# Selection stage of a two-layer encoder kernel: up products over both halves of h at once, in four PSUM banks

## What is computed

```
q  = h @ w_query                                # 8 heads x 128
s1, s2 = q halves times sub_keys                # 128 scores each, per token and head
t1, i1 = top_k(s1, 16);  t2, i2 = top_k(s2, 16)
top_s, top_c = top_k(t1[:, None] + t2[None, :], 16)       # 16 of 256 candidates
experts = i1[top_c // 16] * 128 + i2[top_c % 16];  gates = softmax(top_s)
act = gelu(h . expert_u[experts]);   out = sum(gates * act * expert_v[experts])
```

## Time and profile before

| | us |
|---|---|
| Median of 3 runs (lowest, highest) | 2142.79 (2142.04, 2148.08) |
| The profiled execution | 2141.82 |
| Its span, first to last instruction | 2140.0 |

### The profile page before, as it was taken

The page is one execution under the profiler, slowest core; times in us unless marked ns, Lnnn a source line. Parts: engine busy times, 40 slices in busy tenths (PEclk is TensorE's granted clock), DMA queues, the critical chain, the costliest instruction groups (busy, mean ns, idle before and its releaser), DMA issues.

```text
span 2140.0 us, 38983 instructions
## 1 busy us (share of the span) xinstructions
PE 2045.1 (96%) x12710; PEld 1750.0 (82%) x12710; DVE 1494.8 (70%) x2924; ACT 991.5 (46%) x1651; POOL 665.2 (31%) x548
## 2 busy tenths in 40 slices
PE   7999999988999999999999999998899999999997
PEld 5764899877888999999867549998778899999996
DVE  7882777787778666666678737778877776666665
ACT  4542454575346444444344435446643554444443
POOL 3993466763000000000059916667610000000000
PEclk9999999999999999999999999999999999999998
DMA  5212554203558555555423145542045665555553
GB/s 184 99 70 118 183 173 165 99 21 100 194 190 297 187 186 186 186 187 186 137 95 109 50 160 177 174 159 80 11 152 192 221 196 187 188 186 188 188 186 109
DMA packets 90542, 329.41 MB, mean 154 GB/s; under 512 B 10531, under 2 KB 14755, under 8 KB 88140
## 3 DMA queue, kind: packets, MB, share of 16 engines
q1 hardware_dynamic: 90428, 328.18, 45.2%
q10 hardware_dynamic: 16, 0.02, 0.0%
HBM read 324.99 MB, written 3.16 MB: 153 GB/s over the span
## 4 chain that ended last, share of the span: by engine, by line
PE 73%; POOL 12%; issue 8%; DVE 2%; DMA 2%; ACT 1%; POOLq 1%; DVEq 0%; ACTq 0%; SPq 0%
PE ps L782 33%; PE ps L803 32%; POOL arena L1721 7%; POOL v_raw L1721 3%; PE ps L813 3%; PE ps L746 3%; POOL u_raw L1721 2%; PE ps L698 1%; DVE arena L1259 1%; DMA v_raw<-in_expert_v 1%; PE ps L868 1%; DMA arena<-in_keys 1%; DVE v_hl L1259 1%; PE ps L824 0%; ACT v_hl L1104 0%
## 5 line engine op out<-in xcount | busy, mean ns | idle before, releaser
L803 PE MATMUL ps<-v_hl,w_hl 128*128 128x512 f32 x3072 | 731.0, 393 | 7.5 <-DVE v_hl L1259 7.3
L803 PEld LDWEIGHTS ps<-v_hl,w_hl 128*128 128x128 f32 x3072 | 567.0, 189 | 126.8 <-DVE v_hl L1259 11.2
L782 PEld LDWEIGHTS ps<-h_hl,u_hl 128*128 128x128 f32 x4800 | 598.3, 192 | 12.7
L782 PE MATMUL ps<-h_hl,u_hl 128*128 128x256 f32 x4800 | 608.0, 284 | 0.0
L1721 POOL TENSOR_TENSOR arena<-arena 128x256 f32<-128x256 f32 (+1 forms) x240 | 197.9, 863 | 615.8 <-DVE arena L1259 614.6
L1104 ACT ACTIVATE v_hl<-v_raw 128x1024 fp32r<-128x1024 f32 x208 | 220.8, 1062 | 319.1 <-PE ps L803 292.9
L1259 DVE TENSOR_TENSOR u_hl<-u_raw,u_hl 128x1024 fp32r<-128x1024 f32 x148 | 182.7, 1234 | 188.4 <-ACT u_hl L1066 185.9
L1066 ACT ACTIVATE u_hl<-u_raw 128x1024 fp32r<-128x1024 f32 x144 | 152.9, 1062 | 239.9 <-PE ps L782 239.0
L1259 DVE TENSOR_TENSOR v_hl<-v_raw,v_hl 128x1024 fp32r<-128x1024 f32 x208 | 253.8, 1220 | 12.4 <-ACT v_hl L1104 12.4
L782 PE MATMUL ps<-h_hl,v_hl 128*128 128x256 f32 x1344 | 171.6, 285 | 0.1
L782 PEld LDWEIGHTS ps<-h_hl,v_hl 128*128 128x128 f32 x1344 | 164.8, 192 | 1.7 <-issue 0.5
(11 more groups left out here) (173 smaller groups left out, 2344.7 us busy)
## 6 DMA issues: line engine op xcount, KB each, us to landing
u_raw<-in_expert_u SPq DMA_DIRECT2D x208, 512.0 KB, 3.3
v_raw<-in_expert_v SPq DMA_DIRECT2D x208, 512.0 KB, 3.3
v_raw<-in_expert_u SPq DMA_DIRECT2D x48, 512.0 KB, 4.1
u_raw<-in_expert_v SPq DMA_DIRECT2D x48, 512.0 KB, 3.3
arena<-in_w_in SPq DMA_DIRECT2D x16, 512.0 KB, 3.6
arena<-in_w_in SPq DMA_DIRECT2D x8, 1024.0 KB, 5.1
arena<-in_ssm_b SPq DMA_DIRECT2D x16, 512.0 KB, 4.3
arena<-in_w_out SPq DMA_DIRECT2D x4, 2048.0 KB, 9.6
```

Source lines behind the costliest of these rows:

```text
L782: m = pe.matmul(ps[:, bank, o:o + S], hl[:, wp, k, :], h_hl[:, hp_, k, :], start=(k == 0 and j == 0), stop=(k == DC - 1 and j == 2))
L803: m = pe.matmul(ps[:, 2 * a + half, :], w_hl[s][:, wp, a * P:(a + 1) * P], v_hl[s][:, vp, half * 512:(half + 1) * 512], start=(first and j ...
```

## The change

- **PE** (`up_wide`). The high part of a u slice is multiplied with both halves of `h` by one matmul of 512 columns, into a whole bank: columns 0 to 255 collect high by high, columns 256 to 511 high by low. The low part of the slice adds its 256-column product to columns 0 to 255. An early up product is then 8 matmuls of 512 and 8 of 256 columns, in place of 24 of 256. Each writes one of four banks, and waits for the sum of product `c - 4`. The ahead products stay as they were.
- **ACT** (`half_early`). It copies columns 256 to 511 into row `c` of `gates`. GELU runs three tiles later, in place on that row. The last three GELUs follow behind the last head.
- **DVE** (`pre_early`). It adds columns 0 to 255 to the row. The 48 additions stand between the steps of the selection, six to a head, two tiles behind; the last two stand ahead of the memset that raises `s_topd`.
- The loops on DVE and ACT are turned and unrolled to fit; DVE's loop body now holds two heads.

```diff
 MAG_BANK = 3
+EARLY_BANK = (4, 5, 2, 3)
 TURN_BANK = 0
...
+        def up_wide(c, hl, bank):
+            pe.wait_ge(s_u_lo, l * PK + c + 1)
+            both = ps[:, bank, :].rearrange("p (r t) -> p r t", r=2)
+            def high(k):
+                return pe.matmul(both, hl[:, 0, k, :], h_hl[:, :, k, :], start=(k == 0), stop=(k == DC - 1))
+            high(0)
+            for k in range(DC - 1):
+                pe.matmul(ps[:, bank, 0:S], hl[:, 1, k, :], h_hl[:, 0, k, :], start=False, stop=False)
+                if k < DC - 2:
+                    high(k + 1)
+            pe.matmul(ps[:, bank, 0:S], hl[:, 1, DC - 1, :], h_hl[:, 0, DC - 1, :], start=False, stop=False)
+            high(DC - 1).then_inc(s_u_mm, 1)
         def up_early(c, k):
-            pe.wait_ge(s_gelu, 2 + l * PK + c - 1)
-            up(c, early_hl[k], 4 + k % 2, 0)
+            pe.wait_ge(s_pre_early, l * EARLY + c + 1)
+            up_wide(c, early_hl[k], EARLY_BANK[k])
...
         up_ahead(EARLY + 1, 1, early_hl[1])
+        pe.wait_ge(s_pre_early, 4 + (l + 1) * EARLY)
         pe.wait_ge(s_sel, l + 1)
...
-        def gelu_early(c, s):
+        def half_early(c, k):
+            act.wait_ge(s_u_mm, 2 + l * PK + c + 1)
+            act.activation(gates[:, bass.ds(c, 1), :].rearrange("p o t -> p (o t)"),
+                           ps[:, EARLY_BANK[k], S:2 * S], ACT.Copy).then_inc(s_half, 1)
+        def gelu_early(c):
             act.drain()
-            act.wait_ge(s_u_mm, 2 + l * PK + c + 1)
+            act.wait_ge(s_pre_early, 4 + l * EARLY + c + 1)
             fenced(ACT.Gelu)
-            act.activation(gates[:, bass.ds(c, 1), :].rearrange("p o t -> p (o t)"), ps[:, 4 + s, 0:S],
-                           ACT.Gelu).then_inc(s_gelu, 1)
+            row = gates[:, bass.ds(c, 1), :].rearrange("p o t -> p (o t)")
+            act.activation(row, row, ACT.Gelu).then_inc(s_gelu, 1)
...
                     high_ahead(j - HEAD_UPS + 3)
-                gelu_early(c, j % 2)
+                half_early(c, k % 4)
+                if not first or j >= 3:
+                    gelu_early(c - 3)
                 if following and j == 2:
...
         high_early(2, 2, 0, False)
+        head(0, 0, True, 0, first=True)
         with act.Fori(0, PH // 2 - 1) as hp:
-            head(hp * 2, 0, True, hp * 3)
             head(hp * 2 + 1, 1, True, hp * 3)
-        head(PH - 2, 0, True, 3 * PH // 2 - 3)
+            head(hp * 2 + 2, 0, True, hp * 3 + 3)
         head(PH - 1, 1, False, 3 * PH // 2 - 3, last=True)
+        for c in range(EARLY - 3, EARLY):
+            gelu_early(c)
...
-        with dve.Fori(0, PH) as h:
+        def pre_early(c, k):
+            dve.wait_ge(s_half, l * EARLY + c + 1)
+            row = gates[:, bass.ds(c, 1), :].rearrange("p o t -> p (o t)")
+            tt(row, row, ps[:, EARLY_BANK[k], 0:S], ALU.add).then_inc(s_pre_early, 1)
+        def head(h, s, first):
+            def pre(j):
+                if not first or j >= 2:
+                    pre_early(h * HEAD_UPS + j - 2, (s * HEAD_UPS + j + 2) % 4)
             ih = l * PH + h
...
                 .then_inc(s_sc_used, 1)
+            pre(0)
             dve.drain()
             dve.tensor_copy(i16, i16u)
             tt(cand, t16[:, 0, :, :].unsqueeze(3).broadcast_to([P, TT, 16, 16]),
                t16[:, 1, :, :].unsqueeze(2).broadcast_to([P, TT, 16, 16]), ALU.add)
+            pre(1)
             dve.drain()
             cf = [cand[:, a, :, :].rearrange("p i j -> p (i j)") for a in range(TT)]
             top16(cf, [cand2[:, a, :] for a in range(TT)], [top[:, a, :] for a in range(TT)],
                   [cu[:, a, :] for a in range(TT)])
+            pre(2)
             dve.drain()
...
                top[:, :, 0:1].broadcast_to([P, TT, TOPK]), ALU.subtract)
+            pre(3)
             dve.drain()
             dve.tensor_copy(rank, rank_u)
             dve.drain()
             tt(pick_r, rank_f.unsqueeze(2).broadcast_to([P, 4 * TOPK, TOPK]), over(iota16, 4 * TOPK), ALU.is_equal)
+            pre(4)
             dve.drain()
...
                                   pick[:, b, :, :, :], AX.X, ALU.add)
-            dve.drain()
+            pre(5)
+            dve.drain()
+        dve.wait_ge(s_spill, 16 * (l + 1))
+        head(0, 0, True)
+        with dve.Fori(0, PH // 2 - 1) as i:
+            head(i * 2 + 1, 1, False)
+            head(i * 2 + 2, 0, False)
+        head(PH - 1, 1, False)
+        for c in (EARLY - 2, EARLY - 1):
+            pre_early(c, c % 4)
         dve.memset(fence[:, 2:3], 0.0).then_inc(s_topd, 1)
```

More of the change, by code:

```diff
@@ L317, in encoder @@
         s_gelu = sem("s_gelu")
+        s_pre_early = sem("s_pre_early")
+        s_half = sem("s_half")
         s_wt = sem("s_wt")
@@ L1133, in copy_scores, with head @@
                         .then_inc(s_sc_sb, 1)
-                def head(h, s, following, nth, last=False):
+                def head(h, s, following, nth, last=False, first=False):
                     for j in range(HEAD_UPS):
@@ L1245, in _ @@
             dve.sem_inc(s_gates, 4)
+            dve.sem_inc(s_pre_early, 4)
             for counter in (s_u_mm, s_v_mm, s_gelu, s_pp, s_drive):
```

## The result

The changed kernel takes 2147.16 us (median of 14 runs, 2145.89 to 2149.25), the kernel before 2144.06 us on the same chip (median of 14, 2138.86 to 2148.08). The ratio is 1.0016, with a 95% interval of 1.0009 to 1.0024: it is slower by 3 us. The forecast was 2139.0 us and a small gain. The range held the time, the sign was wrong. The profiled execution of the changed kernel took 2149.25 us, its span is 2147.4 us against 2140.0 before.

A forecast was written before the change was run, and what follows sets the result against it. PE was taken to bound the selection stage. 2141.82 − 9.0 (products) + 5.2 (waits at the end of two layers) = 2138.0 us profiled; with the median 0.97 us above, 2139.0 us was predicted, 8-of-10 range 2132 to 2157.

The forecast's parts named there:

- the sign: Whole kernel: a small gain forecast; chances given were faster 0.20, same 0.55, slower 0.25.
- What bounds the kernel: Selection stage: PE, busy 180.79 of 182 us, sets the pace; DVE has about 4.9 us slack a head.
- PE's part: Early up products: 2786 ns instead of 2880, 94 ns saved each, 9.0 us for 96 products.
- The first rival: Mixed stream of widths saves nothing; products stay at 2.88 us, 2146.7 us in all; chance 0.17.
- the larger saving: Rival on PE's products: fixed matmul cost half hidden, 4.5 us more saved, 2134.5 or 2132 us; chance 0.18.
- DVE's additions: Selection heads: 0.34 us an addition, six make 2.0 us a head, 18.7 us, hidden behind PE's 21.0.
- The end of the stage: Ahead of the transposes: selection ready 8.3 us after product 47, PE waits 2.6 us, 5.2 for two layers.
- The last head: DVE's last head in the selection stage: 20.85 us plus 2.04 for six additions, ending 4.1 us after product 47.
- The chain behind it: After DVE's last head: additions 0.7 us, one GELU 0.48, table load 1.28, exponentials 0.42, then DVE's three steps.
- The exposed table load: End of the selection stage: load for the exponentials, 1.28 us, formerly in DVE's shadow, now behind the last GELU.
- The sum for the profiled execution: Whole kernel: 2141.82 − 9.0 + 5.2 = 2138.0 us.
- The second rival: Selection stage: DVE becomes the bound through losing to POOL; 2167 us, or 2149 if milder; chance 0.25 for both.

The follow-up runs named there:

- x2: Changed kernel with each early up product's eight wide matmuls first, then its eight narrow ones: 2150.61 us, ratio 1.0038 to the kernel before.
- x9: Changed kernel with two small operands of DVE's selection (ranks, first indices) cast into PSUM bank 7: 2131.53 us, ratio 0.9941 to the kernel before.
- x1: Changed kernel with early up products again in 24 matmuls of 256 columns, ACT's copies and DVE's additions kept: 2151.7 us, ratio 1.0032 to the kernel before.
- x5: Changed kernel with s_topd raised before additions 45 to 47, and exponentials before the last three GELUs: 2144.7 us, ratio 1.0007 to the kernel before.
- x4: Changed kernel with eleven idle matmuls of 256 columns ahead of PE's wait for the selection: 2147.91 us, ratio 1.0022 to the kernel before.
- x7: Changed kernel with the last six products of a layer done as before, the other 42 wide: 2134.62 us, ratio 0.9964 to the kernel before.
- x10: Kernel before, with the same two operands in PSUM as x9: 2142.84 us, ratio 0.9992 to the kernel before.
- x12: x9 and x5 together, on the changed kernel: 2134.16 us, ratio 0.9948 to the kernel before.
- x13: x12 with the eight wide matmuls of a product first, as in x2: 2136.86 us, ratio 0.9955 to the kernel before.
- x15: x9 and x7 together, on the changed kernel: 2136.0 us, ratio 0.9951 to the kernel before.

## Why the prediction was wrong, step by step

**What bounds the kernel** held: PE sets the pace, and DVE has little slack left (its heads take 19.6 to 20.6 us in the middle of the stage, up to the end of the reductions, inside the 18.7 to 21.0 us given).

**PE's part** held in kind. The saving is 75 ns a product by the heads (60 by the last two products), not 94. A wide and a narrow matmul in turn take 351 to 352 ns together (an eighth of 2.805 and of 2.82 us; in PE's timeline three pairs in a row begin at 391.33, 391.68 and 392.03), where the rows of the v stage summed to 348.3. Ordered by width, as in x2, the product comes close to 2.786 us. That is 0.9 us a layer less than forecast. The first rival (no saving) is out, and so is the larger saving.

**DVE's additions** held: 0.34 to 0.40 us each. I took the waits out of each head, by comparing each instruction with the shortest of its kind in these traces (1.23 us for the comparison, 1.29 for two products, 0.18 to 0.20 for the small ones):

```
              head length   waits in it   rest
before, 2nd      16.6           1.3       15.3
before, last     20.8           5.5       15.3
after, 2nd       19.7           2.4       17.3
after, last      24.3           7.3       17.0
x9, last         17.6           0.6       17.0
```

The length runs to the end of the reductions, so five of a head's six additions lie in it, and the rest grows by 1.7 to 2.0 us for these five. An addition beside POOL isn't delayed: the one at 385.05 in x9's rows takes 0.41 us while POOL runs.

**The end of the stage is the step that failed**: "PE arrives after 5.76 us and waits 2.6 us". `s_sel` came 10.8 us after product 47 (406.34 − 395.57), not 8.3. The missing 2.5 us lie in these terms of that sum:

- The last head, 1.8 us. I took its old length, 20.85 us, and added six additions: 22.9 us, with its end 4.1 us after product 47. Up to the end of the sixth addition it took 24.6 us (376.89 to 401.48) and ended 5.9 us after. I had priced its waits for POOL as if they were a property of the head; they are one of the phase. Before, DVE waited for two of POOL's instructions nearly in full (2.2 and 2.0 us) and briefly for two more, 5.5 us in all; with the additions in between it waited for three nearly in full (2.2 us each) and briefly for one, 7.3 us. Two of the three long waits fell to a 32-element subtraction and a 64-element cast, which I hadn't counted at all. The trace of the kernel before has such a wait too, in its third head, where it cost PE nothing:

```profile
282.44 2.34 DVE L1259 TENSOR_TENSOR arena<-arena 128x32 f32 x1
```

In x9 the head takes 17.6 us. That run takes the cast, the comparison and the products out of POOL's way; the 32-element subtraction still has both inputs in SBUF and didn't wait because it came in time (384.95, POOL at 385.01). x1 shifts the phase with the same instructions on DVE, and the head takes 21.3 us.
- The chain behind it, 0.7 us: 4.9 us (401.48 to 406.34) instead of 4.2. The additions of 46 and 47 took 0.9 instead of 0.7 us. And I counted one GELU behind the last addition. There are three, since ACT can't do 45 and 46 before DVE's late additions either, and they stand in a row from 401.52 on. Part of that row runs beside the additions of 46 and 47: behind the last addition (402.40) the GELUs end 0.9 us later (403.33), where I had 0.5. x5 shows that they can be moved: with the additions of 45 to 47 also behind the memset, 2.9 us go off the wait ahead of the transposes, and with what comes back behind it the two stretches are 2.2 and 2.0 us shorter. The exposed table load, 1.28 us, was right.

**A term was missing.** Behind the longer wait the granted clock was 0.77 and 0.80 over 8 us, where it had been 1.00, and the transposes with the product behind them took 0.7 us longer in each layer. x4 shows this as the clock's doing.

**The sum for the profiled execution** was −9.0 + 5.2 = −3.8 us. The trace has −7.2 for the products (2 × 3.6), +9.9 for the waits, +1.4 for the clock behind them, +1.5 in the gate stages (nearly all in one), and +1.4 in the rest of the kernel that the change doesn't touch, together +7.0 of the +7.4 us between the spans. The first two alone, at their measured sizes, make +2.7 us, and 3.1 us lie between the medians.

**The second rival** (DVE becomes the bound) had its mechanism right and not its place: POOL and DVE do exclude each other just when the products come, but in the middle of the stage it cost PE nothing (the heads of 19.6 to 20.6 us, with the sixth addition 19.9 to 20.9, stay under PE's 21.1). In x2, which makes PE slightly faster, it did happen. The forecast thus stood on a slack of a quarter of a microsecond in the tightest head, and I should have given the loss at the end a range over the phases: the runs in the same order show 0.7 us of wait a layer (x9, whose last head has 0.6 us of waits), 1.6 (x1) and up to 5.1 (x2).

**What stays open.** The gate stage, which the change doesn't touch, takes 1.4 to 1.8 us longer in both layers of x1 and x4, in x2's first, in x5's first and in the first of the changed kernel, and 2.9 us longer in x5's second, each time with a stretch of low clock in it or at its start. Before, x7, x9, x10, x12, x13 and x15 have a low clock only in its last 4 us if at all, and take 99.6 to 99.7 us. It can't be only what comes ahead: x4 has no more than 0.3 us of wait and no low clock there. No run took its cause apart. Nor is x9's gain fully placed: 13 us by the medians, of which its two selection stages hold 5.2 us; its profiled span is shorter by another 5.2 us between the layers, where nothing was changed and where other kernels vary by a few us as well. Of the 0.6% I count about 0.25% as explained by the stage.

## What to carry to other kernels

When work is added to an engine that excludes another one, don't add it to the old duration of a stretch that held waits: take the waits out, add the work, and then set the waits anew, from none at all to one for each of the partner's instructions that fits in. Price the last round of a pipelined stage apart, with every instruction of the chain that queues up behind the last result (here three GELUs and a table load). And before judging a change by its total, give the engine that it loads its time back, here with two small operands moved to PSUM: what was 0.2% slower became 0.6% faster, of which the traces place 0.25% in the stage.

## What the runs showed of the hardware

- Some of DVE's instructions wait for a POOL instruction of 2.4 us that is running, however small they are: of those with two inputs in SBUF, a subtraction of 32 elements took 2.42 instead of 0.18 us; of those with one input in SBUF and the output there, a cast of 64 elements took 2.36 instead of 0.20 us and (x2) a `TENSOR_SCALAR` of 32 elements 2.39 instead of 0.17. The top-16 instructions and the reductions, SBUF to SBUF too, did so in no trace: in the changed kernel a `FIND_INDEX8` at 388.42 took its usual 0.42 us while POOL ran from 386.55 to 388.96, and x9's reductions at 388.86 took 1.28 us beside POOL. The same cast into PSUM, and the comparison and products with one operand there, ran beside POOL at 0.23 and 1.23 us. The Trainium skill ("SBUF — State Buffer", section SBUF: two separate sides) says that DVE takes the port pair it shares with GpSimd when it has two SBUF inputs, and also when it runs in a 2-port performance mode, as an fp32 copy from SBUF to SBUF does. The trace agrees with the first; the cast and the `TENSOR_SCALAR` fit the second, though no run shows the mode itself. My forecast had used the first condition alone.
- Wide and narrow matmuls in turn, each with its weight load: 351 to 352 ns for 512 + 256 columns, and nearly 348.3 (an eighth of 2.79 us) with the wide ones first. The Trainium skill ("TensorE: Matmul & The Clock Gate", section Back-to-back issue gap) gives N / 2.4 plus about 2.5 ns for an isolated matmul, which makes an estimate of 215.8 + 109.2 = 325 ns; the trace disagrees by 26 to 27 ns a pair, as it did by 10.8 and 12.5 ns at the two widths.
- After PE had been idle for 5.0 us the granted clock was 0.77 and 0.80 over the next two stretches of 4 us (0.59 in one such stretch of the other layer), and six transposes took 1.16 instead of 0.57 us. In x5, with two waits of 2.1 us within 6 us, it was 0.85 and 0.73 from 404 to 412 us; in x1 (1.57 and 0.92 us) and x12 (1.62 us) it stayed at 1.00. Below is a drop in the gate stage of the changed kernel, where PE had been busy for 2.92 of the 4 us ahead (columns as in the earlier trace rows):

```profile
448.00:452.00 4.00, 2.92 (x23) 2.51 (x22) 2.70 (x7) 3.48 (x8) 3.18 (x4) 1.00 0.00 0
452.00:456.00 4.00, 2.93 (x17) 2.74 (x17) 4.00 (x5) 2.08 (x7) 0.84 (x2) 0.74 0.34 114
456.00:460.00 4.00, 4.00 (x31) 4.00 (x31) 2.42 (x5) 1.44 (x4) 3.72 (x4) 0.83 0.06 22
```
